# Causal masks added in PSUM by VectorE in place of matmuls, and quarter splits on GpSimd around a layer's last norm

## The reference

```python
def sb_attend(q, k, v, q_pos, k_pos):
    z = jnp.einsum('bqhd,bkhd->bhqk', q, k).astype(jnp.float32) * SB_SCALE
    visible = k_pos[None, :] < q_pos[:, None]
    log_1mb = jnp.where(visible, jax.nn.log_sigmoid(-z), 0.0)
    suffix = lax.cumsum(log_1mb, axis=3, reverse=True) - log_1mb
    a = jnp.where(visible, jnp.exp(jax.nn.log_sigmoid(z) + suffix), 0.0)
    return jnp.einsum('bhqk,bkhd->bqhd', a.astype(v.dtype), v)

def mla_attend(q_lat, q_rope, c_kv, k_rope, q_pos, k_pos):
    s = (... nope part + rope part) * MLA_SCALE
    visible = (k_pos[None, :] // CHUNK) <= (q_pos[:, None] // CHUNK)
    p = jax.nn.softmax(jnp.where(visible, s, -jnp.inf), axis=-1)
    return jnp.einsum('bhqk,bkl->bqhl', p.astype(c_kv.dtype), c_kv)
```

## Time and profile before

| | us |
|---|---|
| median of 3 runs | 1878.56 (1878.49 to 1878.66) |
| the profiled execution | 1878.33 |
| its span, first to last instruction | 1876.5 |
| PE matmuls busy | 1847.2 |
| VectorE busy | 929.3 |
| ScalarE busy | 558.2 |
| GpSimd busy | 1053.9 |

### The profile page before, as it was taken

One profiled execution on the slowest core, in us unless ns is written; L12 is line 12 of the kernel. 1 busy time (PEld: TensorE's weight loads), 2 busy tenths in 40 slices (PEclk: granted clock), 3 DMA queues, 4 the chain that ended last, 5 costly groups with the idle time before them and its releaser, 6 DMA issues.

```text
span 1876.5 us, 33815 instructions
## 1 busy us (share of the span) xinstructions
PE 1847.2 (98%) x14390; PEld 1782.7 (95%) x14390; DVE 929.3 (50%) x1536; ACT 558.2 (30%) x1164; POOL 1053.9 (56%) x906
## 2 busy tenths in 40 slices
PE   9999999999999999999999999999999999999999
PEld 8998888999999999999999888899999999999988
DVE  6666665331755532524656666652337555235153
ACT  4444443112422221202334344431134222112021
POOL 8585534656455555555566853347465555555543
PEclk9999999999999999999999999999999999999999
DMA  5232111324222222222342321122422222222222
GB/s 186 86 114 69 63 40 57 102 84 156 68 87 83 91 90 90 86 78 92 101 146 86 117 71 46 42 83 84 142 94 68 90 91 86 84 91 91 78 82 93
DMA packets 74806, 168.39 MB, mean 90 GB/s; under 512 B 6112, under 2 KB 33632, under 8 KB 74656
## 3 DMA queue, kind: packets, MB, share of 16 engines
q1 hardware_dynamic: 67328, 158.69, 25.7%
q10 hardware_dynamic: 7328, 7.54, 1.2%
HBM read 156.41 MB, written 9.79 MB: 89 GB/s over the span
## 4 chain that ended last, share of the span: by engine, by line
PE 90%; DVE 6%; ACT 1%; POOL 1%; issue 1%; DMA 1%; SPq 0%; DVEq 0%; ACTq 0%; POOLq 0%
PE ps L1509 74%; PE ps L1544 2%; PE ps L1668 2%; PE ps L1626 2%; PE ps L1718 1%; PE ps L1723 1%; DVE xn L1053 1%; DVE R L1053 1%; DVE xT L1386 1%; DVE mix L1383 1%; PE ps L1583 1%; PE ps L1645 1%; POOL wsp L593 1%; PE ps L1598 1%; DVE xT L1210 1%
## 5 line engine op out<-in xcount | busy, mean ns | idle before, releaser
L1509 PE MATMUL ps<-xn,wsp 128*128 128x272 f32 x7872 | 1009.5, 289 | 9.3 <-issue 5.4
L1509 PEld LDWEIGHTS ps<-xn,wsp 128*128 128x128 f32 x7872 | 991.6, 189 | 14.3 <-issue 10.4
L593 POOL TENSOR_TENSOR wsp<-raw,wsp 128x256 fp32r<-128x256 f32 (+2 forms) x508 | 708.2, 1413 | 22.3
L587 POOL CAST wsp<-raw 128x1024 fp32r<-128x1024 f32 (+2 forms) x354 | 320.4, 917 | 687.8 <-DMA raw<-in_wstream 583.9
L1509 PE MATMUL ps<-R,wsp 128*128 128x272 f32 x3840 | 486.4, 288 | 0.1
L1509 PEld LDWEIGHTS ps<-R,wsp 128*128 128x128 f32 x3840 | 482.9, 189 | 1.4 <-DVE xT L1082 0.5
L1053 DVE SCALAR_TENSOR_TENSOR R<-ps,R 64x256 fp32r<-64x256 f32 (+8 forms) x232 | 127.7, 560 | 84.1 <-ACT R L721 26.8
L1402 DVE TENSOR_TENSOR mix<-ps,rstd 128x272 f32<-128x272 f32 x88 | 38.8, 441 | 202.6 <-PE ps L1509 192.3
L944 ACT ACTIVATE mix<-vv 128x2 f32<-128x2 f32 x88 | 17.9, 204 | 363.0 <-DVE mix L1404 363.0
L1053 DVE SCALAR_TENSOR_TENSOR R<-mix,R 128x544 fp32r<-128x544 f32 (+1 forms) x82 | 71.5, 872 | 81.3 <-ACT R L965 66.9
L1410 DVE SCALAR_TENSOR_TENSOR ps<-mix,vv,ps 128x546 f32<-128x546 f32 x88 | 69.4, 789 | 55.6 <-ACT ps L953 55.6
(11 more groups left out here) (225 smaller groups left out, 1478.9 us busy)
## 6 DMA issues: line engine op xcount, KB each, us to landing
raw<-in_wstream SPq DMA_DIRECT2D x233, 512.0 KB, 3.7
raw<-in_wstream SPq DMA_DIRECT2D x48, 128.0 KB, 2.7
raw<-in_wstream SPq DMA_DIRECT2D x16, 384.0 KB, 3.1
raw<-in_kc SPq DMA_DIRECT2D x8, 512.0 KB, 4.0
raw<-in_vc SPq DMA_DIRECT2D x8, 512.0 KB, 4.2
xT<-in_x_in SPq DMA_DIRECT2D x8, 272.0 KB, 5.1
out_k_out<-mix ACTq DMA_DIRECT2D x8, 272.0 KB, 3.2
xT<-in_x_in SPq DMA_DIRECT2D x1, 2176.0 KB, 8.2
```

The costliest lines, as they stand in the source:

```text
L587: ins = nc.gpsimd.tensor_copy(dst[:, 0, f], part[:, f])
L593: ins = nc.gpsimd.tensor_tensor(dst[:, 1, f], part[:, f], dst[:, 0, f].bitcast(F32), ALU.subtract)
L1509: mm = pe.matmul(z[:, h], w[:, x, (k0 + k) * P:(k0 + k + 1) * P], rhs[:, y, k, h * HT:(h + 1) * HT], start=(k == 0 and (x, y) == (0, 0)), ...
```

## The change

For s units the two mask matmuls go. VectorE gets mask(s) at the head of its step: it waits for z_done, adds a 128 x 128 mask to the last 128 columns of both heads in PSUM, and raises a new count, z_masked, for which ScalarE's sigmoids wait in place of z_done. The triangle has to lie the other way round for this, so in layer 0 PE multiplies it once with the identity after q0 (into bank 6, columns 384 to 511), VectorE copies the result to masks[:, 3] between rope_rotate and the evacuation of q0, and PE waits for this copy before k0.

For m units the two matmuls go as well, and VectorE writes -1e30 into the 64 x 64 block per head that isn't visible (a memset on 64 partitions, with a wait of its own) ahead of the maxima.

In STREAM the chunks ("K", 1) and ("qr", 1) change places. In FILL step 14 gets a third quarter (the last of ga0), which step 15 loses. On GpSimd the chunks from ("down", 2, 4) on, which are four of 768 floats, pp1 and the eight pleg, are split with the finer pieces too. PE's first matmuls wait for the second memset instead of the first.

```diff
@@ -57,7 +57,7 @@
 STREAM = [("c", 0), ("kr", 0), ("q", 0), ("k", 0), ("v", 0), ("v", 1), ("q", 1), ("k", 1), ("ukuv", 0), ("qr", 0),
-          ("v", 2), ("q", 2), ("k", 2), ("K", 0), ("K", 1), ("qr", 1), ("v", 3), ("V", 0), ("V", 1), ("q", 3), ("k", 3),
+          ("v", 2), ("q", 2), ("k", 2), ("K", 0), ("qr", 1), ("K", 1), ("v", 3), ("V", 0), ("V", 1), ("q", 3), ("k", 3),
           ("qn", 0), ("ga", 0), ("gb", 0), ("K", 2), ("K", 3), ("qn", 1), ("ga", 1), ("V", 2), ("V", 3), ("gb", 1),
@@ -290,7 +290,7 @@
                        ("ga", 1), ("gb", 1), ("qn", 2), ("qn", 3), ("ga", 2), ("gb", 2), ("ga", 3), ("gb", 3)],
-                      [4, 4, 4, 3, 3, 3, 4, 4, 3, 4, 4, 4, 3, 2, 2, 3, 3, 3] +
+                      [4, 4, 4, 3, 3, 3, 4, 4, 3, 4, 4, 4, 3, 2, 3, 2, 3, 3] +
                       [2, 2, 1, 2, 1, 2, 2, 2, 1, 1, 2, 2, 1, 1, 2, 2, 2, 4, 0])
...
@@ -580,7 +580,7 @@
                             pool.wait_ge(S["x_add"], 2 * KT)
-                        fine = c <= ST_AT[("proj", 1)]
+                        fine = c <= ST_AT[("proj", 1)] or c >= ST_AT[("down", len(FFN_PARTS) - 1, 4)]
                         n_hi = 2 if fine and w == CW else 1
@@ -795,7 +795,10 @@
                         pos, neg = rtok[:, R_POS, i:i + 1], rtok[:, R_NEG, i:i + 1]
-                        act.wait_ge(S["z_done"], s + 1)
+                        if br == "s":
+                            act.wait_ge(S["z_masked"], [u[0] for u in units[0:s + 1]].count("s"))
+                        else:
+                            act.wait_ge(S["z_done"], s + 1)
                         if s >= 2:
...
@@ -1197,6 +1200,15 @@
 
+                    def mask(s):
+                        br, t, qb = units[s]
+                        if br == "s":
+                            dve.wait_ge(S["z_done"], s + 1)
+                            if s == 0 and layer == 0:
+                                dve.wait_ge(pre["mask_set"], 1)
+                            z = z_view(s, P * (qb + 1))[:, :, qb * P:(qb + 1) * P]
+                            v.tensor_tensor(z, z, masks[:, 3].unsqueeze(1).broadcast_to((P, 2, P)), ALU.add).then_inc(S["z_masked"], 1)
+
                     def suffixes(s):
@@ -1241,6 +1253,7 @@
                             n = slice(2 * i, 2 * i + 2)
+                            link(v.memset(z_view(s, P * (qb + 1))[0:CHUNK, :, P * qb + CHUNK:P * (qb + 1)], NEG))
                             link(v.reduce_max(negmax[:, n], z_view(s, P * (qb + 1)), mybir.AxisListType.X))
@@ -1282,6 +1295,10 @@
                     rope_rotate(0, ("kr", 0))
+                    if layer == 0:
+                        dve.wait_ge(pre["made"], 2)
+                        dve.wait_ge(pre["mask_turned"], 1)
+                        v.tensor_copy(masks[:, 3], ps[:, 6, 3 * P:4 * P]).then_inc(pre["mask_set"], 1)
                     qk_tile(("q", 0))
@@ -1300,6 +1317,7 @@
                         if s < NS:
+                            mask(s)
                             suffixes(s)
...
@@ -1580,11 +1598,8 @@
                             for r in range(2):
-                                pe.matmul(ps[:, ZB + 2 * (n % 2) + r, 0:w], qk[64 * r:64 * r + 64, t % 2, 0, x, qb * P:(qb + 1) * P],
-                                          qk[64 * r:64 * r + 64, t % 2, 1, y, 0:w], start=(i == 0), stop=False, skip_group_check=True)
-                        for r in range(2):
-                            mm = pe.matmul(ps[:, ZB + 2 * (n % 2) + r, qb * P:w], masks[:, 1], ident_b, start=False, stop=True,
-                                           skip_group_check=True)
+                                mm = pe.matmul(ps[:, ZB + 2 * (n % 2) + r, 0:w], qk[64 * r:64 * r + 64, t % 2, 0, x, qb * P:(qb + 1) * P],
+                                               qk[64 * r:64 * r + 64, t % 2, 1, y, 0:w], start=(i == 0), stop=(i == 2), skip_group_check=True)
                         mm.then_inc(S["z_done"], 1)
@@ -1720,10 +1735,8 @@
                                 a = 64 * (t % 2) + 32 * r
-                                pe.matmul(z[:, r], qr[a:a + 32, x, t // 2, qb * P:(qb + 1) * P], krT[a:a + 32, y, 0:w],
-                                          start=False, stop=False, tile_position=(a, 0), skip_group_check=True)
-                        for r in range(2):
-                            mm = pe.matmul(z[:, r, qb * P:w], ident_b, masks[:, 2], start=False, stop=True, skip_group_check=True)
+                                mm = pe.matmul(z[:, r], qr[a:a + 32, x, t // 2, qb * P:(qb + 1) * P], krT[a:a + 32, y, 0:w],
+                                               start=False, stop=(i == 2), tile_position=(a, 0), skip_group_check=True)
                         mm.then_inc(S["z_done"], 1)
@@ -1796,13 +1809,18 @@
                     project(("q", 0), ("q", 0), xn, KT)
+                    if layer == 0:
+                        pe.wait_ge(pre["made"], 2)
+                        pe.wait_ge(pre["logs"], 1)
+                        pe.matmul(ps[:, 6, 3 * P:4 * P], masks[:, 1], ident_b, start=True, stop=True,
+                                  skip_group_check=True).then_inc(pre["mask_turned"], 1)
                     pe.wait_ge(S["c_sq"], 1)
                     rstd_turn(("rt", 0))
+                    if layer == 0:
+                        pe.wait_ge(pre["mask_set"], 1)
                     project(("k", 0), ("k", 0), xn, KT)
                     project(("v", 0), ("v", 0), xn, KT)
-                    if layer == 0:
-                        pe.wait_ge(pre["made"], 2)
                     for s in range(STEPS):
```

More of the change, by code:

```diff
@@ L439, in build @@
                  "sq_done acc_done rstd_done xn_used rt_set c_sq k_scaled xn_hi xn_lo r_mul x_add sq2_done sq2_sum zeroed "
-                 "v_raw v_st k_raw k_st "
-                 "z_done w_done b_done r_done a_done at_tr at_hi at_lo "
+                 "v_st k_raw k_st "
+                 "z_done z_masked w_done b_done r_done a_done at_tr at_hi at_lo "
                  "ones_set cache_used "
@@ L449, in build @@
             pre = {n: st.enter_context(nc.semaphore(n)) for n in
-                   ("con_in", "late_in", *(f"x_in{k}" for k in range(KT)), "c_in", "half_hi", "half_lo", "cleared", "made", "eps_made", "squares", "added", "summed", "logs", "roots",
+                   ("con_in", "late_in", *(f"x_in{k}" for k in range(KT)), "c_in", "half_hi", "half_lo", "mask_turned", "mask_set", "made", "eps_made", "squares", "added", "summed", "logs", "roots",
                     "y_st")}
@@ L1022, in _ @@
             def _(dve):
-                nc.vector.memset(rstd[:], 0.0).then_inc(pre["cleared"], 1)
+                nc.vector.memset(rstd[:], 0.0)
                 nc.vector.memset(epsb[:], EPS).then_inc(pre["eps_made"], 1)
@@ L1468, in _ @@
             def _(pe):
-                pe.wait_ge(pre["cleared"], 1)
+                pe.wait_ge(pre["eps_made"], 1)
                 for k in range(KT):
```

## The result

The changed kernel takes 1881.01 us, the median of 14 runs (1878.26 to 1883.29); the kernel before, timed beside it, 1877.92 us (1876.1 to 1880.36). The ratio is 1.0017, with a 95% interval of 1.0009 to 1.0024: slower by 0.17%. The forecast of 1877.5 us was on the wrong side of it. The time lies inside the stated range and inside the 0.2% that was named as the bound of no change, but the loss is clear of its interval.

What follows compares the result with a forecast made beforehand. TensorE (PE), busy for 98% of the span, was taken as the bound. Against the profiled 1878.33 us, gains of 10.2 and losses of 9.4 gave 1877.5 us; the range, 8 times in 10, was 1872.8 to 1882.0.

Steps and rivals of the forecast that it cites:

- The clock behind the new waits: Clock falls behind new waits at k0 and steps 3 and 12: one counted, 1.7 us lost; none to three possible.
- Rival (c): Slower through VectorE's queue: delays over 1.9 us, or falls behind all four double waits, 1882.6 us; chance 0.15.
- steps 3 and 12: Sigmoids in both layers wait behind VectorE's evacuation of k1/k3: 1.36 us each, 5.4 lost; bounds 0.2 to 1.8 per place.
- qr1 ahead of K1: PE's wait for qr1 in step 7 goes: 1.0 us gained in layer 0, 0 in layer 1 because of q3.
- k0: Layer 0: PE waits for VectorE's copy of the transposed mask, so k0 starts at 33.7; 2.3 us lost.
- the stop ahead of gb0: Step 15, both layers: PE's stop for VectorE's evacuation of kv0 goes, 1.1 us each; 2.2 us gained.
- the norms: Last norm of each layer: the addition of squares shrinks beside quarter splits; 0.8 us a layer, 1.6 gained, bounds 0 and 3.6.
- the pair's price: Two mask matmuls of one unit removed from PE: 0.085 us a pair, 38 pairs, 3.2 us gained.
- The fall at layer 1's last norm: The granted clock's fall to 0.52 after that norm's wait goes with the shorter wait; 1.7 us gained.
- Step 16: Scans no longer beside GpSimd's split of qn1, which comes earlier: 0.25 us a layer, 0.5 us gained.
- Rival (b): Mask matmuls worth more, evacuation ahead of the sigmoid costing less: 1873.1 us at 0.2 us a pair; chance 0.15.
- rival (d): Change doesn't do what it says, e.g. gb0 still waits: each loses 1 to 2 us; no chance of its own.

Runs made afterwards that it cites:

- run 1: Changed kernel with VectorE's masks of steps 3 and 12 moved ahead of the low halves of k1 and k3; 1872.0 us, 0.9973 of the kernel before.
- run 4: Changed kernel with the edits of run 1 and run 2 together; 1869.15 us, 0.9959 of the kernel before.
- run 6: run 4 with K1 ahead of qr1, as before the change; 1869.55 us.
- run 5: run 3 with K1 ahead of qr1, as before the change; 1869.85 us, 0.9953 of the kernel before.
- run 3: Changed kernel with stick-breaking masks by PE matmuls again, without the transposed mask and its copy; 1874.62 us, 0.9982 of the kernel before.
- run 10: run 4 with some 128 more PE instructions, long-met waits in layer 0's out projections, to move an instruction fetch; 1871.27 us.
- run 2: Changed kernel with the transposed mask made behind k0 and copied behind k0's low half, PE not waiting ahead of k0; 1878.76 us.
- run 7: run 4 with the filling quarter of step 14 back in step 15; 1872.73 us.
- run 8: run 4 with GpSimd's splits around the last norm as whole chunks again; 1870.71 us.
- run 9: run 5 with the latent masks by PE again as well; 1871.0 us.
- run 11: Changed kernel with VectorE masks only in stick-breaking steps 1, 5, 6, 7, 10, 14, 15, run 2's late copy and run 5's order; 1867.96 us, ratio 0.9945.

## Why the prediction was wrong

The forecast had a gain of 0.8 us, the medians show a loss of 3.1. Its mechanisms were nearly all there; it failed mostly on sizes, and three terms and one omission carry the miss. The sizes below are those of the profiled execution.

**The clock behind the new waits**, 1.7 us forecast, 4.3 in the profiled execution. The step that failed is "one wait in two of such a length had a fall behind it, so I count one fall". That came from two waits of 1.9 us; of the five new waits, the four of steps 3 and 12 had three falls, each 3 us at 0.50, and the one ahead of k0 had none. By the timed runs the number of falls differs between executions: the mean clock goes from 0.999 to 0.997, and the medians of run 1 and of the changed kernel are 9.0 us apart where waits and three falls would be 11.2. Rival (c), the slower side, named this mechanism and its place (all four falls, 1882.6) and was given 0.15: it is what happened in the profiled execution, with three falls in place of four. What decides whether a wait has a fall behind it stays open.

**The waits of steps 3 and 12**, 5.4 forecast, 6.9 measured. The delay of the sigmoid was right to 0.01 us. What was left out is that a delayed operation meets other neighbours: in step 3 of layer 0 the scans took 3.18 us in place of 2.71 beside GpSimd's split. The bound of 1.8 us a place held in layer 1 (1.67 and 1.52) and was passed in layer 0 (1.82 and 1.90).

**qr1 ahead of K1**, 1.0 gained by forecast, 0.3 lost. "Layer 0 keeps 1.0 of the 1.3 us" took GpSimd's end of q3 (129.87) as fixed and PE's slack of 1.05 us as free. But v3's load waits for PE, which at that point still had the whole delay of step 3 (5.3 us): GpSimd started v3 5.55 us later than before and ended q3 5.90 later, where PE, with the wait ahead of qr1 gone, was by then only 3.85 later. Runs 4 and 6 show that the order gives nothing; between runs 5 and 3 it cost 4.8 us, a part of it by the fetch named above.

**The wait ahead of v0 in layer 1**, 0.9 us, was in no term. Taking PE instructions out shifts the fetches of them; in run 10, where the fetch was moved, this wait was gone.

Right were: k0 (2.3 forecast, 2.25 in run 2's medians and in the trace; it started at 33.52, forecast 33.7), the stop ahead of gb0 (2.2 against 2.3, and run 7 gave 3.6 with step 16), the norms (1.6 against 1.8, and run 8 gave 1.6), and the pair's price: 3.2 forecast, 2.6 in the trace. The fall at layer 1's last norm (1.7) is gone as forecast, but that may be luck: run 8 has waits of 1.71 and 1.65 us at the two norms and no fall. Run 9 refuted two other prices of a pair, its busy time of 0.28 us and 0.162, twice the 81 ns that the Trainium skill gives ("TensorE: Matmul & The Clock Gate", section "Back-to-back issue gap"): by that estimate the 26 pairs would have been 4.2 us, where 1.15 was measured. Step 16 gained 1.2 where 0.5 was forecast. Rival (b) fell with the pair's price; of rival (d) nothing was seen: the change does what it says at each place.

The rule of the Trainium skill in "SBUF — State Buffer", section "SBUF: two separate sides", that VectorE is locked out for GpSimd's whole instruction, fits what was measured: the addition of squares is 1.14 us beside subtractions by quarters and 2.31 to 2.50 beside a whole chunk.

The sum of the gains, without VectorE's queue, was there to be had: the kernel before with nothing but the filling quarter and the norms' quarters (run 9) takes 1871.0 us, 0.9961 of it. The masks on VectorE, the largest part of the diff, give 3.0 us more at their best: 1.15 for the latent ones (run 5 against run 9) and 1.9 for seven of the stick-breaking steps of a layer (run 11 against run 5).

## What to carry to other kernels

Moving a small operation to an idle engine is judged by what stands ahead of it in that engine's queue at that moment, not by the engine's share of busy time: here 0.4 us of VectorE work, placed behind an evacuation, cost 1.5 to 1.9 us each time and 1.4 to 1.5 more where the clock fell, and placed ahead of it left 0.2 (run 1: PE waits 0.49 us ahead of step 3's transposes, 0.27 in the kernel before). When a wait is removed, follow the producer that PE will meet next, and ask whether its own start was set by PE before or behind the gain. Where a change opens new waits, count the clock as a cost of its own, in the slower direction first: five new waits had three falls here.

## What the runs showed of the hardware

A wait of PE of 1.3 to 2.7 us was followed by some 3 us at half the clock in some places and not in others, and up to 1.95 us the length of the wait doesn't tell them apart. With a fall: the last norm of layer 1 in the kernel before (1.90 us), step 3 of layer 0 and step 12 of both layers in the changed kernel and in run 2 (1.3 to 1.7 us and then 0.58, with the scores between), and q3 in both layers of runs 3 and 10 (2.39 and 2.52, 1.35 and 2.69). Without one, among others: the last norm of layer 0 in the kernel before (1.90), k0 (1.95) in the changed kernel, step 3 of layer 1 in it and in run 2 (1.51 and 1.45, then 0.58), q3 in layer 0 of run 1 (1.34), both norms of run 8 (1.71 and 1.65). The timed runs of the changed kernel spread over 5 us, nearly in order of their mean granted clock. The profiled executions of runs 1, 4 to 9 and 11 have a mean clock of 1.000.

A fetch of PE's instructions is a DMA transfer, and it competes with the loads of weights, as far as these times show it. The page counts 113 of them, 1.85 MB, 16 KB each, for 14263 matmuls and as many weight loads, so one for about 250 instructions (with PE's semaphore waits it is 256, the median between two fetches in the trace). Where one stood 0.2 or 0.3 us behind the issue of v3's four loads (runs 3 and 10, layer 1), the issue took 3.4 us in place of 2.5 and the split started 6.9 and 7.2 us behind it, in layer 1 of the other kernels 5.1 to 5.9. Where one stood 6.5 us behind the issue of v0's eight loads, the split started 9.7 to 10.0 us behind it; with the fetch 3 to 6 us ahead of the loads (the kernel before, runs 9 and 10) it was 8.2 to 8.3, with the fetch 0.6 ahead (runs 3 and 5) 8.6 and 9.2, and with the fetch 3.5 behind (run 11) 9.1, without a wait of PE. So taking instructions out, or putting in waits that are long met, can move a stall from one place to another. That the queues of the DMA engines are the cause is argued from these records; the only thing tried was moving the fetch.
